# A float32 transformer block on one core: down products of the feed-forward part filled and drained by column halves, with five seven-product pairs a stage

## The reference, cut to what matters

```python
z = rmsnorm(h, norm2_w) @ mlp_w1            # 2048 -> 8192
h = h + jnp.square(jax.nn.relu(z)) @ mlp_w2 # 8192 -> 2048
...
h = rmsnorm(h, final_norm_w)
```

## Time and profile before

| | |
|---|---|
| median of three runs | 2070.66 us (2070.02 to 2074.72) |
| the profiled execution, its own time | 2069.63 us |
| its span, first to last instruction | 2067.8 us |
| TensorE busy | 98% of the span |
| VectorE busy | 72% |
| ScalarE busy | 61% |
| loads | 182 GB/s on average |

### The profile page before, as it was taken

How to read it: one execution, slowest core, us unless ns; L and a number is a source line. 1 busy time by engine, 2 the same in 40 slices (tenths; PEclk the granted TensorE clock), 3 DMA queues, 4 the chain that set the end, 5 groups by cost and what they waited for, 6 DMA issues and landing times.

```text
span 2067.8 us, 25757 instructions
## 1 busy us (share of the span) xinstructions
PE 2026.5 (98%) x9838; PEld 1707.5 (83%) x9838; DVE 1483.3 (72%) x1974; ACT 1259.7 (61%) x1855; POOL 6.1 (0%) x12
## 2 busy tenths in 40 slices
PE   9999999999999999999999999999999899999998
PEld 7888888888898888888899988887778678777886
DVE  6665565857977777658866578878857876886664
ACT  7666667646566777556666455576447546644754
POOL 0000000000000000000000000000000000000000
PEclk9999999999999999999999999999999999999999
DMA  8766554555556554556555465665656555556664
GB/s 264 206 192 197 171 157 149 191 186 189 193 178 191 156 155 152 196 179 197 177 169 158 123 187 185 188 194 166 203 172 192 180 185 174 182 175 192 210 202 148
DMA packets 198879, 375.48 MB, mean 182 GB/s; under 512 B 13875, under 2 KB 48917, under 8 KB 198230
## 3 DMA queue, kind: packets, MB, share of 16 engines
q1 hardware_dynamic: 198758, 373.85, 58.3%
HBM read 371.71 MB, written 2.10 MB: 181 GB/s over the span
## 4 chain that ended last, share of the span: by engine, by line
PE 94%; DVE 4%; ACT 1%; issue 1%; DMA 0%; SPq 0%; ACTq 0%
PE acc L580 23%; PE acc L582 23%; PE acc L581 23%; PE acc L1082 3%; PE acc L1085 2%; PE acc L1084 2%; PE acc L986 2%; PE acc L988 2%; PE acc L987 2%; PE acc L831 1%; PE tp L592 1%; PE acc L809 1%; DVE wlo L1826 1%; ACT whi L1212 1%; PE tp L831 1%
## 5 line engine op out<-in xcount | busy, mean ns | idle before, releaser
L1826 DVE TENSOR_TENSOR wlo<-raw,whi 128x1024 fp32r<-128x1024 f32 x597 | 724.2, 1222 | 411.6 <-ACT whi L1212 408.1
L1212 ACT ACTIVATE whi<-raw 128x1024 fp32r<-128x1024 f32 x615 | 647.8, 1060 | 517.0 <-PE acc L582 368.8
L580 PE MATMUL acc<-whi,both 128*128 128x512 f32 (+1 forms) x592 | 226.4, 382 | 0.0
L582 PE MATMUL acc<-whi,both 128*128 128x512 f32 (+1 forms) x592 | 224.6, 379 | 0.0
L581 PE MATMUL acc<-wlo,both 128*128 128x512 f32 (+1 forms) x592 | 224.4, 379 | 0.0
L580 PE MATMUL acc<-whi,bT 128*128 128x512 f32 x512 | 200.3, 391 | 7.1 <-DVE x L2619 7.1
L580 PE MATMUL acc<-whi,aT 128*128 128x512 f32 x508 | 200.1, 394 | 0.0
L582 PE MATMUL acc<-whi,bT 128*128 128x512 f32 x512 | 199.7, 390 | 0.0
L581 PE MATMUL acc<-wlo,bT 128*128 128x512 f32 x512 | 199.7, 390 | 0.0
L582 PE MATMUL acc<-whi,aT 128*128 128x512 f32 x508 | 198.1, 390 | 0.0
L581 PE MATMUL acc<-wlo,aT 128*128 128x512 f32 x508 | 197.8, 389 | 0.0
(11 more groups left out here) (458 smaller groups left out, 3655.5 us busy)
## 6 DMA issues: line engine op xcount, KB each, us to landing
raw<-in_mlp_w SPq DMA_DIRECT2D x256, 512.0 KB, 4.0
raw<-in_w_in_a SPq DMA_DIRECT2D x128, 512.0 KB, 3.8
raw<-in_w_ple_gate SPq DMA_DIRECT2D x64, 512.0 KB, 4.1
raw<-in_w_in SPq DMA_DIRECT2D x64, 512.0 KB, 3.9
raw<-in_w_in_b SPq DMA_DIRECT2D x40, 512.0 KB, 3.9
raw<-in_w_out_a SPq DMA_DIRECT2D x32, 512.0 KB, 4.1
raw<-in_w_out_b SPq DMA_DIRECT2D x32, 512.0 KB, 4.4
raw<-in_w_out SPq DMA_DIRECT2D x32, 512.0 KB, 4.5
```

Source lines behind the costliest of these rows:

```text
L580: pe.matmul(o, hi[:, kt, tok], whi[:, slot, wc], start=start, stop=False)
L582: mm = pe.matmul(o, lo[:, kt, tok], whi[:, slot, wc], start=False, stop=stop)
L1212: act.activation(whi[:, u % RING, 0:n], raw[:, u % RING, 0:n], ACT.Copy).then_inc(hi_done, 1)
L1826: dve.tensor_tensor(wlo[:, u % RING, 0:n], raw[:, u % RING, 0:n], whi[:, u % RING, 0:n].bitcast(F32), ALU.subtract).then_inc(lo_done, 1)
```

## The change

- FAST becomes ((3, 5), (1, 3, 5)): pairs 3 and 5 in chunk 0, pairs 1, 3 and 5 in chunk 1, five in a stage. The sums of z tiles are made for the pairs 1, 3, 5.
- The first and the last pair of units of each chunk are common ones, and their products are ordered by column halves: both units into acc[0], then both into acc[1]. `down_half` is signalled when the last pair has finished acc[0].
- VectorE adds acc[0] into x at step 13 and acc[1] at step 14 (`chunk_added`), and combines the shared banks later (`shared_hooks`): for chunk 0 at steps 0 to 3 of chunk 1, for chunk 1 at steps 3 to 6 of the next up stage.
- The square of z is a second pass of ScalarE on `zN` in place; VectorE's L2587 goes. A bank of the up stage is free when the Relu has read it.
- The sums of a pair's weights wait for the loads alone and are made ahead of the first unit's low half, one dependent add after the other; they are split one unit earlier (`sums_due(u, 2)`).

```diff
-FAST = (0, 2, 4)
+FAST = ((3, 5), (1, 3, 5))
+SUMMED = sorted(set(FAST[0] + FAST[1]))
...
                     if j == 0:
-                        pe.wait_ge(sem("up_out"), 4 * q + 3 + i)
+                        pe.wait_ge(sem("up_relu"), TT * (4 * q + 2 + i) + t + 1)
                     else:
                         pe.wait_ge(sem("down_d"), 4 * (n - 1) + 2 * i + t + 1)
...
+                    elif kp in (0, s.units // 2 - 1):
+                        last = kp > 0
+                        unit_ready(one)
+                        both_tokens(one, 0)
+                        unit_ready(two)
+                        mm = both_tokens(two, 0, last)
+                        if last:
+                            mm.then_inc(sem("down_half"), 1)
+                        both_tokens(one, 1).then_inc(unit_used, 1)
+                        both_tokens(two, 1, last).then_inc(unit_used, 1)
+                        sums_products(one)
+                        sums_products(two)
...
                     for t in range(TT):
                         act.activation(zN[:, t, :], acc[(s.c0 + j) % 2][t][:, :], ACT.Relu, scale=rs[:, RS["norm2"], t:t + 1]).then_inc(sem("up_relu"), 1)
+                    for t in range(TT):
+                        act.wait_ge(sem("up_relu"), TT * (4 * q + j) + t + 1)
+                        act.activation(zN[:, t, :], zN[:, t, :], ACT.Square).then_inc(sem("z_squared"), 1)
...
             def quad_summed(u, g):
-                slot, sums = u % RING, quad[g % 2]
-                four = quarters(u)
-                dve.wait_ge(hi_done, u + 2)
+                sums, four = quad[g % 2], quarters(u)
                 if g >= 2:
                     dve.wait_ge(sem("quad_used"), g - 1)
+                for v in (u, u + 1):
+                    dve.wait_ge(raw_full[v % RING], raw_count(v))
                 dve.tensor_tensor(sums[:, 0:2, :], four[:, 0:4:3, :], four[:, 1:2, :].to_broadcast((P, 2, CH)), ALU.add).then_inc(sem("quad_step"), 1)
-                dve.tensor_tensor(wlo[:, slot + 1, :], raw[:, slot + 1, :], whi[:, slot + 1, :].bitcast(F32), ALU.subtract)
                 dve.wait_ge(sem("quad_step"), 2 * g + 1)
                 dve.tensor_tensor(sums[:, 2, :], sums[:, 0, :], four[:, 3, :], ALU.add).then_inc(sem("quad_step"), 1)
-                dve.tensor_tensor(wlo[:, slot, 0:CH], raw[:, slot, 0:CH], whi[:, slot, 0:CH].bitcast(F32), ALU.subtract).then_inc(lo_done, 1)
                 dve.wait_ge(sem("quad_step"), 2 * g + 2)
-                dve.tensor_tensor(sums[:, 3, :], sums[:, 2, :], four[:, 2, :], ALU.add).then_inc(lo_done, 1)
+                dve.tensor_tensor(sums[:, 3, :], sums[:, 2, :], four[:, 2, :], ALU.add).then_inc(sem("quad_sums"), 1)
...
+            def shared_hooks(n, at):
+                return {at: [lambda: product_sums(n)], at + 1: [lambda: more_sums(n)], at + 2: [lambda: first_tokens(n)], at + 3: [lambda: last_tokens(n)]}
+
+            def chunk_added(q, j, i):
+
+                n = 2 * q + j
+                if i:
+                    ended(S[f"down{q}"], j)
+                else:
+                    dve.wait_ge(sem("down_half"), n + 1)
+                    if q:
+                        dve.wait_ge(sem("pair_x"), 2 * (n - 1))
+                for t in range(TT):
+                    xq = x[:, t, (2 * j + i) * CH:(2 * j + i + 1) * CH]
+                    dve.tensor_tensor(xq, xq, acc[i][t][:, :], ALU.add).then_inc(sem("down_d"), 1)
+
             def z_out(q, j):
-                n, c = 4 * q + j, S[f"up{q}"].c0 + j
-                for t in range(TT):
-                    dve.wait_ge(sem("up_relu"), TT * n + t + 1)
-                    m = dve.scalar_tensor_tensor(out=zN[:, t, :], in0=acc[c % 2][t][:, :], scalar=rs[:, RS["norm2"], t:t + 1], in1=zN[:, t, :],
-                                                 op0=ALU.mult, op1=ALU.mult)
-                m.then_inc(sem("up_out"), 1)
-                dve.wait_ge(sem("up_out"), n + 1)
+                n = 4 * q + j
+                dve.wait_ge(sem("z_squared"), TT * (n + 1))
                 dve.wait_ge(sem("moved"), P // BLK * MOVED.index((f"z{q}", j)))
                 flipped(zN, 0, 1)
...
-                        hooks = {} if q else join({q - 1: [lambda q=q: blocks_turned("x5", 3, q)] for q in (2, 3)},
+                        hooks = shared_hooks(2 * q - 1, 3) if q else join({q - 1: [lambda q=q: blocks_turned("x5", 3, q)] for q in (2, 3)},
...
+                    along(s, j, join(shared_hooks(2 * q, 0) if j else z_lo(q, 3),
+                                     {13: [lambda q=q, j=j: chunk_added(q, j, 0)], 14: [lambda q=q, j=j: chunk_added(q, j, 1)]}))
```

More of the change, by code:

```diff
@@ L1099, in pair_of_chunks, with unit_ready @@
+                def unit_ready(uu):
                     if j == 0 and uu % QT == 0:
                         pe.wait_ge(sem("split_lo"), MOVED.index((f"z{q}", uu // QT)) + 1)
[L1101 to L1104, removed]
+                    pe.wait_ge(lo_done, s.u0 + j * s.units + uu + 1)
@@ L1105, in pair_of_chunks @@
+                for kp in range(s.units // 2):
+                    one, two = 2 * kp, 2 * kp + 1
+                    if kp in FAST[j]:
+                        i = SUMMED.index(kp)
+                        unit_ready(one)
                         if n == 0:
@@ L1108, in pair_of_chunks @@
                             pe.wait_ge(sem("p1_out"), n)
[L1109 to L1112, removed]
+                        three(tp[0], zt, tokens(one, 0), *weights(one, 0), kp == FAST[j][-1]).then_inc(unit_used, 1)
+                        sums_products(one)
+                        unit_ready(two)
@@ L1113, in pair_of_chunks @@
                         bank_free(0, 0)
-                        three(acc[0][0], zt, tok[0], whi[:, slot, cols[0]], wlo[:, slot, cols[0]], False)
+                        three(acc[0][0], zt, tokens(two, 0), *weights(two, 0), False)
+                        pe.wait_ge(sem("zs_lo"), summed_before(q, kp) + 1)
                         bank_free(1, 0)
-                        mm = three(acc[1][0], zs, (slice(None), i, 3), whi[:, slot, cols[1]], wlo[:, slot, cols[1]], False)
-                    else:
-                        last = uu == s.units - 1
-                        for i in range(2):
-                            for t in range(TT):
[L1121 to L1134, removed]
-                        three(acc[0][1], zt, (slice(None), kt, slice(P, 2 * P)), t_hi[:, 3, :], t_lo[:, 3, :], False)
-                        three(xb[0], zs, (slice(None), i, 0), t_hi[:, 0, :], t_lo[:, 0, :], last)
-                        three(tp[1], zs, (slice(None), i, 1), t_hi[:, 2, :], t_lo[:, 2, :], last)
-                        three(xb[1], zs, (slice(None), i, 2), t_hi[:, 1, :], t_lo[:, 1, :], last).then_inc(sem("quad_used"), 1)
+                        three(acc[1][0], zs, (slice(None), i, 3), *weights(two, 1), False).then_inc(unit_used, 1)
@@ L2607, in _ @@
                 for j in range(2 if q < PAIRED else 0):
-                    n, cols = 2 * q + j, slice(2 * j * CH, 2 * (j + 1) * CH)
-                    along(s, j, join({} if j else z_lo(q, 3), {12: [lambda: product_sums(n)], 13: [lambda: more_sums(n)],
-                                                               14: [lambda: first_tokens(n, cols)], 15: [lambda: last_tokens(n, cols)]}))
-                    dve.wait_ge(sem("pair_x"), 2 * n + 2)
-                    for i in range(2):
-                        if i:
-                            ended(s, j)
-                        else:
-                            dve.wait_ge(sem("down_half"), n + 1)
-                        for t in range(TT):
-                            xq = x[:, t, (2 * j + i) * CH:(2 * j + i + 1) * CH]
-                            dve.tensor_tensor(xq, xq, acc[i][t][:, :], ALU.add).then_inc(sem("down_d"), 1)
+                    along(s, j, join(shared_hooks(2 * q, 0) if j else z_lo(q, 3),
+                                     {13: [lambda q=q, j=j: chunk_added(q, j, 0)], 14: [lambda q=q, j=j: chunk_added(q, j, 1)]}))
                 for j in range(3 if q == PAIRED else 0):
```

128 lines of the change are left out of this document (83 added, 45 removed).

## The result

The changed kernel takes 2046.79 us (median of 4 runs, 2046.2 to 2047.38) against 2070.46 us for the kernel before beside it: a ratio of 0.9881, 95% interval 0.9864 to 0.9898. That is 23.7 us less; 2045.9 was forecast. The profiled execution has a span of 2045.6 us.

The account below looks back on a forecast made before the run. TensorE, busy 98%, bounds the kernel, so only product count and stalls matter. 42.3 us removed, 2.0 added for products and 15.5 for new waits: 24.8 less, 2070.66 to 2045.9 us; range 2036 to 2058.

Parts of the forecast that it names:

- The 42.3 us lost before: TensorE's stalls in three paired down stages, 13.6 us each, plus 1.5 us once at up2's start; all removed.
- All five gaps: TensorE idle in down1: 1.67 at the start, 1.03 and 1.31 for low halves, 4.11 between chunks, 2.36 before up2.
- the gap at the down start: 1.67 us at a down stage's start; goes, since acc[1] is free at 1.46 against 2.72 us of cover.
- The gap of 1.03: In down1, TensorE waits 1.03 us for a unit whose low half isn't ready.
- the square's move: z's square on ScalarE, two passes of 0.6 us: hidden in all 16 chunks, with VectorE's flips starting at 2.53, not 3.17.
- The new waits: Six late units a paired stage behind VectorE's queue, in chunks 0 and 1: 5.2 us a stage, 15.5 in all.
- 0.1 us for the first product after a gap: Price of each old TensorE gap: idle time plus 0.16 for overlap, plus this 0.1.
- the longer step: VectorE's dependent adds start 0.04 us after the previous end; the skill's view would save 1.6 us in all.
- The ring: Rival: the four-unit ring absorbs all VectorE bursts, only 9 products are paid; 40.3 us less, 2030.4; chance 0.12.
- further behind: Rival: VectorE at 92% in chunk 1 hands on every slip, waits twice the forecast; 2061.4 us; chance 0.20.
- The clock didn't fall: Rival: each of 18 new waits brings seven half-clock products, 1.4 us more; 2071.1, or 2086.6 with doubled waits; chance 0.03.
- the change did what it says: Rival denied here: banks still late at one of three boundaries, 2 us a stage; 2052 us; chance 0.05.

Follow-up runs that it names:

- all the moves, z's low part at step 8: Changed kernel, VectorE reordered: chunk 0's shared sums at step 13, their adds at 9 and 10, z's low part at 8, sums' low half one unit later; 2032.63 us.
- the same with step 6: The kernel with VectorE's queue reordered, with z's low part at step 6 of chunk 0 instead of step 8; 2031.34 us, ratio 0.9802.
- the reordered kernel with six pairs: The kernel with VectorE's queue reordered and z's low part at step 6, with the sixth pair back in chunk 0; 2044.05 us, ratio 0.9867.
- six pairs: The changed kernel with FAST = ((1, 3, 5), (1, 3, 5)), the sixth pair back, 9 products fewer; 2054.94 us, ratio 0.9923.

## Why the prediction was right

**The 42.3 us lost before.** All five gaps of the earlier trace rows went, as forecast: the window's clock is back at 1.00 and no product at a border waits. The chain of causes was tested from both sides: with the sums put back the gaps between the chunks and before the next up stage return (2081), without the half ordering 1.2 us a stage do, and with the sums put off but the pairs left at the borders a gap of the same length opens elsewhere (2071). For the gap at the down start two parts of the change are each enough, as said. The gap of 1.03 has `issue` in its bracket in the earlier trace rows; that it was a wait for a low half follows from VectorE's timeline, where that low half ends at 1617.35, 0.09 ahead of the product:

```profile
1616.66 0.69 DVE L1849 TENSOR_TENSOR wlo<-raw,whi 128x512 fp32r<-128x512 f32 x1
```

**The start of a down stage.** The Relu passes and the squares, ScalarE's timeline at down1:

```profile
1598.57 1.27 ACT L1817 ACTIVATE zN<-acc,rs 128x512 f32<-128x512 f32 x2 [1.60 <-PE acc L591]
1599.72 1.15 ACT L1820 ACTIVATE zN<-zN 128x512 f32<-128x512 f32 x2
1600.77 1.06 ACT L1250 ACTIVATE whi<-raw 128x1024 fp32r<-128x1024 f32 x1
```

From the first product at 1598.37 the Relus end at 1.47 (1.46 forecast), the next rounding starts at 2.40 (2.4). No table load stands at the squares. What I had wrong is a small sign: I called the square's move hidden and counted the earlier flips as its effect; against VectorE doing it, with the rest of the change in place, it costs 0.14 us a stage.

**The new waits.** This is the step that carries the number. VectorE's queue by hand and as it ran, from the timeline at down1:

```profile
1605.06 1.23 DVE L1868 TENSOR_TENSOR wlo<-raw,whi 128x1024 fp32r<-128x1024 f32 x1 [1.74 <-ACT whi L1250]
1606.32 1.79 DVE L1948 STREAM_TRANSPOSE mov<-zN 32x256 f32<-32x256 f32 x4
1608.14 1.22 DVE L1868 TENSOR_TENSOR wlo<-raw,whi 128x1024 fp32r<-128x1024 f32 x1
1609.40 1.80 DVE L1948 STREAM_TRANSPOSE mov<-zN 32x256 f32<-32x256 f32 x4
1611.23 1.23 DVE L1887 TENSOR_TENSOR quad<-raw 128x1024 f32<-128x1024 f32 x1
1612.49 0.69 DVE L1889 TENSOR_TENSOR quad<-quad,raw 128x512 f32<-128x512 f32 x1
1613.21 0.69 DVE L1891 TENSOR_TENSOR quad<-quad,raw 128x512 f32<-128x512 f32 x1
1613.82 0.68 DVE L1859 TENSOR_TENSOR wlo<-raw,whi 128x512 fp32r<-128x512 f32 x1
1614.42 1.22 DVE L1961 TENSOR_TENSOR both<-mov,both 128x1024 fp32r<-128x1024 f32 x1
1615.56 2.35 DVE L1868 TENSOR_TENSOR wlo<-raw,whi 128x1024 fp32r<-128x1024 f32 x2
```

Less 1598.37, units 4 and 5 start at 6.69 and 9.77 (forecast 6.70, 9.69), the sums at 12.86 (12.66), and unit 7's low half ends at 18.41 (18.22). The waits of down1, as start to start less the pitch of 0.23, were 1.45, 0.25, 0.11, 1.67, 0.90 and 0.26; forecast 1.27, 0.41, 0.14, 1.83, 1.09, 0.41. All six were where the queue said, in all three stages. Each forecast holds 0.06 us from the end of the low half to the product, which the prediction adds without saying so; in unit 7 of chunk 0 it was 0.05 (the low half ends at 1616.78, the product starts at 1616.83).

**The term that was mis-sized.** For the gaps before I had added 0.1 us for the first product after a gap; for the new ones I forgot it. 18 x 0.11 = 2.0 us. The waits themselves were 4.6 us a stage and not 5.15, 13.9 in all. A further 0.2 us a stage stands in no single place: it is spread over products that start 0.24 after the one ahead instead of 0.23. Together 16.5 us (89.2 less 83.7 in each stage) where 15.5 was forecast. The rest of the profile's distance (2045.6 against 2043.0) lies ahead of the feed-forward part: down0's first product is at 1422.1 us, before at 1420.2, in code that didn't change, with the single wait of 1.0 at L589 among it. Two kernels of this study that are alike up to there have it at 1421.6 (all the moves, z's low part at step 8) and 1420.1 (the same with step 6), so it is scatter between executions. The medians differ by 23.7 us, and the stages explain 7.4 + 7.6 + 7.2 = 22.2, and 1.5 us of slow clock after down1 the remainder. That the term came within 1.0 us is partly luck: the waits were 1.5 us shorter than forecast, and 2.6 us beside them had been left out. The medians also agree better (0.9 us) than the profiled spans (2.6 us), since the profiled execution was the slowest of its four.

**Dependent adds.** The sums in the lines above start 1.26 and 0.72 apart, while a half-width pass that waits for nothing follows after 0.61 (1613.21 to 1613.82). So the longer step was right. The Trainium skill ("VectorE: DVE Perf Modes", The DRAIN you can't avoid) has the two alike; in this kernel a pass that waits for the one ahead costs 0.12 us more than one that doesn't, 0.24 a pair, and the measurement decides. (The prediction wrote the start after the end as 0.04 us in one place and 0.03 in another; it is 0.03, 1611.23 + 1.23 against 1612.49.)

**The rivals.** The ring doesn't absorb the bursts in this order; in a better one it does (2031). VectorE isn't "further behind": the waits were 4.6 us a stage and not twice 5.2. Of that rival's mechanism, load in chunk 1, the runs show that work of 87% of the products' time hides there without a wait; the 92% of the changed kernel were not tried in a better order, so for them it stays open. The clock didn't fall after any of the new waits, 1.52 us at most. The margin is small: in the reordered kernel with six pairs two idle times of 1.55 and 1.60 us, 5.7 us of products between them, brought it down once in three stages. Where it fell in the experiments it took 7 to 11 products with it, my price had seven. And the change did what it says at all three borders.

## What to carry to other kernels

Where one in-order engine feeds and empties another, write its queue down with the traced durations and mark when each result is wanted: six waits of a new order came out within 0.2 us each. Busy share doesn't tell load from order: 14 us came, with the same instructions, from moving steps that nobody was waiting for behind those that somebody was, or into a stretch in which the engine stood idle. A drain that is put off needs a place where nothing urgent stands ahead of its own consumers; alone it only moves the gap. A cheaper product scheme pays only where the engines that make its operands have room: the sixth pair saves TensorE 0.68 us a stage and made the stage 2.9 us longer in one order and 3.3 to 5.3 in the other.

## What the runs showed of the hardware

TensorE's clock and the idle time ahead of it, over all kernels here (half level: products 0.43 apart and 0.63 long, which is 1.2 GHz; full level 0.23 apart):

| idle before | where | half level after it |
|---|---|---|
| 4.1 to 5.75 us | the kernel before (4.11), the one with the sums not put off (5.75 and 4.2), the one with putting off alone (4.19) | 12 of 12 |
| 2.9 | six pairs | in 3 of 3, in one of them only 1.5 us after the gap |
| 2.36 | before the next up stage, kernel before | 1 of 3 |
| 1.55 and 1.60 with 5.7 us of products between | six pairs in the new order | 1 of 3 |
| 1.67 and less | all others, the changed kernel among them (1.52 at most) | never |

So the same gap can cost its length alone or more than that, within one execution: the 2.36 before up2 cost 1.5 us on top, the same gap before the two other up stages nothing. Over all these cases the half level took 1.3 to 2.1 us. What decides whether it comes, these runs don't show. TensorE's timeline in the six-pair kernel, in the stage where it came late:

```profile
1614.85 0.41 PE L1094 MATMUL acc<-whi,both 128*128 128x512 f32 x1
1615.09 0.61 PE L1091 MATMUL acc<-whi,both 128*128 128x512 f32 x1
1615.49 0.63 PE L1093 MATMUL acc<-wlo,both 128*128 128x512 f32 x1
```

The gap ended at 1613.59; six products ran at the full level, and then the level fell while TensorE was busy. By these rows, in a budget a gap of some 2.4 us or more should be given a price above its length.
